# A mixed attention and mLSTM block: norms' row and gate columns through device memory, one turn for each small table

## The reference

```
h    = rms_norm(x, pre_norm_g)                       # one reciprocal norm for each token
proj = h @ w_in                                      # aq ak av az | mq mk mv mo mz | mi mf
ya   = moba_attention(partial_rope(aq), partial_rope(ak), av)
ya   = rms_norm(ya, attn_out_g) * silu(az)
qk   = silu(causal_depthwise_conv([mq, mk], conv_w, conv_b))
hm   = mlstm(q, k * 128**-0.5, mv, mi + i_bias, mf + f_bias)
       # lf = log_sigmoid(mf), running sums of lf, running maxima m_t,
       # weights exp(b_t - b_s + i_s - m_t), denominators max(|n q|, exp(-m_t))
ym   = sigmoid(mo) * layer_norm(hm) * mlstm_out_g * silu(mz)
x    = x + rms_norm([ya, ym] @ w_out, post_norm_g)
```

## Time and profile before

| | before |
|---|---|
| median of 3 runs | 317.78 us (317.5 to 318.87) |
| profiled execution: first to last instruction | 316.2 us |
| PE busy (matmul) | 309.4 us, 98% |
| DVE busy | 225.4 us, 71% |
| ACT busy | 165.2 us, 52% |
| POOL busy | 95.9 us, 30% |
| DMA, mean over the span | 121 GB/s |

### The profile page before, as it was taken

One profiled execution on the slowest core, in us unless ns is written; L12 is line 12 of the kernel. 1 busy time (PEld: TensorE's weight loads), 2 busy tenths in 40 slices (PEclk: granted clock), 3 DMA queues, 4 the chain that ended last, 5 costly groups with the idle time before them and its releaser, 6 DMA issues.

```text
span 316.2 us, 4992 instructions
## 1 busy us (share of the span) xinstructions
PE 309.4 (98%) x1599; PEld 256.4 (81%) x1599; DVE 225.4 (71%) x508; ACT 165.2 (52%) x336; POOL 95.9 (30%) x118
## 2 busy tenths in 40 slices
PE   8999999999999999999999999999999999999992
PEld 4888888888888888888888888778888888888882
DVE  2544999748998699968998568964577766856534
ACT  3548857287345324663157563384556876353301
POOL 8201006056350213002320025592711984000000
PEclk9999999999999999999999999999999999999999
DMA  7941553956725486645864332210220473310111
GB/s 222 323 99 38 153 149 93 170 163 150 134 68 146 134 158 205 188 124 122 180 227 151 102 90 77 73 66 31 67 68 0 125 200 145 133 68 0 68 66 67
DMA packets 29081, 38.30 MB, mean 121 GB/s; under 512 B 3624, under 2 KB 15184, under 8 KB 29056
## 3 DMA queue, kind: packets, MB, share of 16 engines
q1 hardware_dynamic: 27424, 34.51, 36.2%
q0 software_dynamic: 1472, 3.34, 7.0%
q10 hardware_dynamic: 160, 0.14, 0.1%
HBM read 33.68 MB, written 4.29 MB: 120 GB/s over the span
## 4 chain that ended last, share of the span: by engine, by line
PE 93%; issue 3%; DMA 2%; DVE 0%; DVEq 0%; SPq 0%; ACT 0%; POOLq 0%; POOL 0%; ACTq 0%
PE bank L1476 24%; PE bank L1478 24%; PE bank L1477 24%; PE bank L1814 3%; PE bank L1524 3%; PE bank L1758 3%; PE bank L1779 3%; PE bank L1612 2%; DMA farena<-in_x 2%; PE bank L1708 1%; PE bank L1505 1%; PE bank L1769 1%; PE bank L1613 1%; PE bank L1552 1%; PE bank L1551 1%
## 5 line engine op out<-in xcount | busy, mean ns | idle before, releaser
L778 ACT ACTIVATE w_hi<-w_raw 128x512 fp32r<-128x512 f32 x71 | 43.7, 626 | 63.2 <-PE bank L1478 51.1
L1476 PE MATMUL bank<-w_hi,xT_hi 128*128 128x512 f32 (+1 forms) x180 | 72.5, 403 | 0.0
L1478 PE MATMUL bank<-w_hi,xT_lo 128*128 128x512 f32 (+1 forms) x180 | 69.8, 388 | 0.0
L1477 PE MATMUL bank<-w_lo,xT_hi 128*128 128x512 f32 (+1 forms) x180 | 69.3, 385 | 0.0
L1043 DVE TENSOR_TENSOR w_lo<-w_raw,w_hi 128x512 fp32r<-128x512 f32 x64 | 45.5, 721 | 11.1 <-ACT w_hi L778 11.0
L1476 PE MATMUL bank<-xT_hi,w_hi 128*128 128x512 f32 x128 | 50.8, 397 | 0.0
L1478 PE MATMUL bank<-xT_hi,w_lo 128*128 128x512 f32 x128 | 50.1, 392 | 0.0
L1477 PE MATMUL bank<-xT_lo,w_hi 128*128 128x512 f32 x128 | 50.0, 390 | 0.0
L1478 PEld LDWEIGHTS bank<-w_hi,xT_lo 128*128 128x128 f32 x180 | 33.8, 188 | 7.2
L1476 PEld LDWEIGHTS bank<-w_hi,xT_hi 128*128 128x128 f32 x180 | 33.9, 188 | 5.8 <-issue 0.4
L1477 PEld LDWEIGHTS bank<-w_lo,xT_hi 128*128 128x128 f32 x180 | 34.0, 189 | 5.5
(11 more groups left out here) (211 smaller groups left out, 581.8 us busy)
## 6 DMA issues: line engine op xcount, KB each, us to landing
w_raw<-in_w_in SPq DMA_DIRECT2D x72, 256.0 KB, 2.9
w_raw<-in_w_out SPq DMA_DIRECT2D x16, 256.0 KB, 2.7
kq_rows<-stage SPq DMA_DIRECT2D x8, 256.0 KB
gy<-kq_rows SPq DMA_DIRECT2D x8, 256.0 KB, 3.5
gy<-in_x SPq DMA_DIRECT2D x4, 512.0 KB, 5.4
out_y<-gy SPq DMA_DIRECT2D x7, 256.0 KB, 2.1
farena<-in_x SPq DMA_DIRECT2D x4, 256.0 KB, 5.3
farena<-in_x SPq DMA_DIRECT2D x2, 512.0 KB, 7.5
```

The costliest lines, as they stand in the source:

```text
L778: a.activation(hi, raw, ACT.Copy).then_inc(w_hi_done, 1)
L1476: pe.matmul(o, hi, m_hi, start=start, stop=False)
L1477: pe.matmul(o, hi, m_lo, start=False, stop=False)
L1478: return pe.matmul(o, lo, m_hi, start=False, stop=stop)
```

## The change

Four things change, and no arithmetic on the result does.

1. **Norms' row.** PE turns `rx` (128 x 4) once into four rows, DVE copies 4 x 128 values, and POOL writes them to device memory, waits, and reads the row back into all partitions of `rbc`. `rbc_done` is now the landing of that DMA.
2. **Gate steps.** The multiplication of the gate rows by `rbc` (`gate_scale`) moves on DVE from ahead of slots 10 to 14 to step 8, behind the cuts of slots 12 to 14. ACT's three first gate steps (`gate_first`) move in the same way into step 8. PE waits for the small copy and no more for `rbc` before slot 10.
3. **Rotation table.** One turn of the whole table (128 x 128) takes the place of four; ACT's copy out of PSUM is 128 x 128; POOL writes it to device memory with four DMAs instead of one.
4. **Gate columns.** PE's four turns and DVE's copy are gone. SP, at slot 20, waits for the gate rows and issues five small DMAs to device memory; at slot 22 it waits for them and issues one DMA that reads back 32 values for each of 128 partitions, with neighbours 512 bytes apart in memory. ACT's exponential in step 18 and the decays wait for that DMA.

The semaphores' declarations and one repeated wait are left out of the diff.

```diff
@@ -87,6 +87,7 @@
 P_AT = [0, 512, 896, 1152]
 NU = NT * AH
+COLS_OUT, COLS_BACK = 20, 22
@@ -253,8 +254,8 @@
         pcol = sb("pcol", [P, R_END])
         wg_raw = sb("wg_raw", [P, NK, 8])
         wg = sb("wg", [P, NK, P], F32R)
-        aT = sb("aT", [P, NT, 16])
-        emt = sb("emt", [P, NT, MH])
+        gate_col = sb("gate_col", [P, 2 * NT * MH])
+        emt = sb("emt", [P, MH, NT])
         ssx = sb("ssx", [P, NT])
         msx = sb("msx", [P, NT])
         rx = sb("rx", [P, NT])
@@ -312,7 +313,7 @@
         bcol = pcol[0:16, R_BIAS:R_END]
         by_dims, whole = stage, gate
         rope_t = [f_part(F_COS, SEQ), f_part(F_SIN, SEQ)]
-        rope_flat = f_part(F_SIN, SEQ)[0:2 * ROT, :]
+        rope_flat = f_part(F_SIN, P)
         def by_block_order(ap):
             return ap.rearrange("p (m h j) -> p h m j", m=4, h=AH)
@@ -358,6 +359,8 @@
         kq_dram = nc.dram_tensor("kq_rows", (2, AH, DH, SEQ), F32, kind="Internal").ap()
         rope_dram = nc.dram_tensor("rope_rows", (2, ROT, SEQ), F32, kind="Internal").ap()
         g_dram = nc.dram_tensor("g_rows", (16, SEQ), F32, kind="Internal").ap()
+        rx_dram = nc.dram_tensor("rx_row", (1, SEQ), F32, kind="Internal").ap()
+        col_dram = nc.dram_tensor("col_rows", (2 * NT * MH, P), F32, kind="Internal").ap()
         x_in = [sem(f"x_in{c}") for c in range(len(X_CHUNKS))]
@@ -548,6 +553,19 @@
                 sp.dma_start(dst, src).then_inc(raw_in[n % RAW], 16)
                 if n == NK - 1:
                     sp.dma_start(wg_raw[:], w_in[0, :, MG:MG + 8].rearrange("(k p) c -> p k c", p=P)).then_inc(wg_in, 16)
+                if n == COLS_OUT:
+                    sp.wait_ge(gdiff_done, 1)
+                    sp.wait_ge(gneg_done, 1)
+                    for j in range(NT):
+                        rows_of_tile = slice(MH * j, MH * (j + 1))
+                        sp.dma_start(col_dram[rows_of_tile, :], gate_rows[rows_of_tile, j * P:(j + 1) * P])\
+                            .then_inc(cols_out, 16)
+                    sp.dma_start(col_dram[NT * MH:, :].rearrange("(h j) p -> h (j p)", j=NT), gate_rows[32:32 + MH, :])\
+                        .then_inc(cols_out, 16)
+                if n == COLS_BACK:
+                    sp.wait_ge(cols_out, 16 * (NT + 1))
+                    with nc.allow_non_contiguous_dma(reason="a column per row"):
+                        sp.dma_start(gate_col[:], col_dram.rearrange("g p -> p g")).then_inc(cols_back, 16)
                 if n == S_QK + 6:
                     sp.wait_ge(ssx_done, NT)
                     sp.dma_start(gains[:], attn_g.to_broadcast([P, AW])).then_inc(gain_in, 16)
@@ -637,6 +655,10 @@
             g.wait_ge(consts, 1)
             g.wait_ge(msx_done, 1)
             rsqrt(rx[:], msx[:]).then_inc(rx_done, 1)
+            g.wait_ge(rx_row_done, 1)
+            g.dma_start(rx_dram.rearrange("o (t p) -> (o t) p", p=P), rbc[0:NT, 0:P]).then_inc(rx_out, 16)
+            g.wait_ge(rx_out, 16)
+            g.dma_start(rbc[:], rx_dram.to_broadcast([P, SEQ])).then_inc(rbc_done, 16)
             g.wait_ge(gmax_done, 1)
             g.tensor_tensor(rows[4], rows[1], rows[2], ALU.subtract).then_inc(grows_done, 1)
@@ -680,8 +702,10 @@
             decay_rows(0)
             decay_mask(0)
             g.wait_ge(rope_flat_done, 1)
-            g.dma_start(rope_dram.rearrange("q j s -> (q j) s"), rope_flat).then_inc(rope_out, 16)
-            g.wait_ge(rope_out, 16)
+            for t in range(NT):
+                g.dma_start(rope_dram.rearrange("q j s -> (q j) s")[:, t * P:(t + 1) * P],
+                            rope_flat[t * 2 * ROT:(t + 1) * 2 * ROT, :]).then_inc(rope_out, 16)
+            g.wait_ge(rope_out, 16 * NT)
             for q in range(2):
                 g.dma_start(rope_t[q], rope_dram[q:q + 1].to_broadcast([AH, ROT, SEQ])).then_inc(rope_spread, 16)
             for t in range(NT):
@@ -816,16 +840,18 @@
             for t in range(NT):
                 mv_high(t)
-            a.wait_ge(gate_sb, 1)
-            a.activation(rows[0], gate_rows[32:48, :], ACT.Abs, bias=bcol[:, 1:2]).then_inc(absf_done, 1)
-            a.wait_ge(absf_done, 1)
-            a.activation(rows[1], rows[0], ACT.Exp, scale=-1.0).then_inc(expf_done, 1)
-            a.activation(rows[6], gate_rows[0:16, :], ACT.Identity, bias=bcol[:, 0:1]).then_inc(igate_done, 1)
+            def gate_first():
+
+                a.wait_ge(gate_sb, 1)
+                a.activation(rows[0], gate_rows[32:48, :], ACT.Abs, bias=bcol[:, 1:2]).then_inc(absf_done, 1)
+                a.wait_ge(absf_done, 1)
+                a.activation(rows[1], rows[0], ACT.Exp, scale=-1.0).then_inc(expf_done, 1)
+                a.activation(rows[6], gate_rows[0:16, :], ACT.Identity, bias=bcol[:, 0:1]).then_inc(igate_done, 1)
             def decays(h, j):
                 a.wait_ge(g_masked, NT * h + j + 1)
-                a.activation(decay[j], decay[j], ACT.Exp, bias=aT[:, j, 4 * j + h:4 * j + h + 1])\
+                a.activation(decay[j], decay[j], ACT.Exp, bias=gate_col[:, NT * j + h:NT * j + h + 1])\
                     .then_inc(decay_done, 1)
             def rope_scale():
@@ -838,7 +864,7 @@
             def rope_evac():
                 a.wait_ge(rope_ps, 1)
-                a.activation(rope_flat, bank[6][0:2 * ROT, :], ACT.Copy).then_inc(rope_flat_done, 1)
+                a.activation(rope_flat, bank[6][:, 0:P], ACT.Copy).then_inc(rope_flat_done, 1)
             def conv_silu(n):
                 a.wait_ge(conv_done, n + 1)
@@ -892,6 +918,7 @@
                         v_copy(t)
                 cut(b + AHEAD)
                 if b == S_QK:
+                    gate_first()
                     a.wait_ge(onep_done, 1)
                     a.activation(rows[0], rows[2], ACT.Ln).then_inc(ln_done, 1)
                 if b == S_QK + 1:
@@ -902,9 +929,8 @@
                     a.wait_ge(gmax_done, 1)
                     a.activation(gate_rows[32:48, :], rows[2], ACT.Copy, scale=-1.0).then_inc(gneg_done, 1)
                 if b == ST_AT[0]:
-                    a.wait_ge(aT_done, 1)
-                    a.activation(emt[:], bank[7][:].rearrange("p (t c) -> p t c", t=NT)[:, :, 32:32 + MH],
-                                 ACT.Exp).then_inc(emt_done, 1)
+                    a.wait_ge(cols_back, 16)
+                    a.activation(emt[:].rearrange("p h t -> p (h t)"), gate_col[:, NT * MH:], ACT.Exp)                        .then_inc(emt_done, 1)
                 for h in range(MH):
                     if b - 2 in PE_ST and PE_ST[b - 2][0] == h:
                         pm_high(*PE_ST[b - 2])
@@ -1085,18 +1111,21 @@
             v.tensor_scalar(rx_fourth[:], rx[:], 0.25, None, ALU.mult).then_inc(rx_half_done, 1)
             cut(RING)
             cut(RING + 1)
-            v.wait_ge(rbc_ps, 1)
-            v.tensor_copy(rbc[:], bank[5][:]).then_inc(rbc_done, 1)
-            v.wait_ge(rbc_done, 1)
+            v.wait_ge(rx_turned, 1)
+            v.tensor_copy(rbc[0:NT, 0:P], bank[5][0:NT, 0:P]).then_inc(rx_row_done, 1)
             v.wait_ge(par_done, 2)
             v.wait_ge(consts, 4)
             v.wait_ge(gate_split, 1)
             link(v.tensor_tensor(gate_rows, bank[7][0:P // 2, :], gate_low_rows, ALU.add))
-            v.tensor_tensor(gate_rows, gate_rows, rbc[0:P // 2, :], ALU.mult).then_inc(gate_sb, 1)
             cut(RING + 2)
             cut(RING + 3)
             for t in range(NT):
                 mv_low(t)
+
+            def gate_scale():
+
+                v.wait_ge(rbc_done, 16)
+                v.tensor_tensor(gate_rows, gate_rows, rbc[0:P // 2, :], ALU.mult).then_inc(gate_sb, 1)
             def gate_low():
@@ -1196,7 +1225,7 @@
                 for q in range(2):
                     v.bn_stats(bns[:, q, :], pv[:, q, 0:MD])
-                link(v.scalar_tensor_tensor(out=den[:], in0=pv[:, :, MD], scalar=-1.0, in1=emt[:, t0:t0 + 2, h],
+                link(v.scalar_tensor_tensor(out=den[:], in0=pv[:, :, MD], scalar=-1.0, in1=emt[:, h, t0:t0 + 2],
                                             op0=ALU.mult, op1=ALU.max))
                 link(v.tensor_tensor(den[:], pv[:, :, MD], den[:], ALU.max))
                 for q in range(2):
@@ -1271,15 +1300,12 @@
                     head_sum(*PE_PV[b - 2])
                 cut(b + AHEAD)
                 if b == S_QK:
+                    gate_scale()
                     gate_low()
                 if b == S_QK + 1:
                     gate_sums()
                 if b == S_QK + 2:
                     gate_maxima()
-                if b == S_QK + 6:
-                    v.wait_ge(gcol_ps, 1)
-                    v.tensor_copy(aT[:], bank[7][:].rearrange("p (t c) -> p t c", t=NT)[:, :, 0:16])\
-                        .then_inc(aT_done, 1)
                 for c in range(2):
                     for m in (2 * c, 2 * c + 1):
                         if b == S_AQ - 3 + (m > 0):
@@ -1562,25 +1588,13 @@
                 pe.wait_ge(rx_done, 1)
                 pe.wait_ge(xt_lo, NK)
```

(28 more changed lines are left out.)

## The result

| | before | after |
|---|---|---|
| median | 318.05 us (6 runs) | 325.31 us (6 runs, 324.4 to 327.15) |
| ratio of the runs | | 1.023, 95% interval 1.021 to 1.0251 |
| profiled execution, its span | 316.2 us | 325.4 us |
| profiled execution, its time | | 327.15 us |
| chain that ended last, share of PE | 93% | 79% |

The changed kernel is slower by 7.3 us, 2.3%. The forecast had the sign, the place and the chain of links, and half of the size (+3.6 us). The profiled execution is the slowest of the six, 1.8 us above their median, so its gap is larger than that of the median run. Of all executions behind the numbers of this document, one of ten of e3_rope_turn took 344.06 us at a mean granted clock of 0.851, and its ratio leaves that one out.

What follows compares the result with a forecast made beforehand. PE bounds the kernel, level with the gate chain at 69.7 us. Weighting end 69.62 + 2.3 (maxima) - 0.1 (copy gone) + 1.4 (columns) = 73.2, so +3.6: 321.4 us, range 318.9 to 325.5.

Steps and rivals of the forecast that it cites:

- the sign: Whole kernel: slower, median 317.78 + 3.6 = 321.4 us; slower given 0.80.
- the place: PE ahead of score tile 1 of head 0: waits some 4 us for the weighting of tile 0.
- the chain of links: Norms' row, gate steps, maxima, slot 24's issue and landing, ACT's decays, DVE's weighting: end moves from 69.62 to 73.2 us.
- The term of the sum for the gate columns: SP's queue at slot 22: the column read delays slot 24's landing by 1.4 us.
- the clock: Rival: PE idle about 4.5 us lets the clock fall, adding some 2 us, 323.5 us; chance 0.2, with costlier columns.
- the time at the rotation table: PE's turn after slot 11: may stall 0.5 us (none to 1.8), taken in by the later wait.
- T: Landing of the norms' row in `rbc` through device memory: 40.1 us, with ends 39.35 and 41.35.
- The maxima: DVE's gate maxima end at T+10.5, 50.6 us instead of 48.29, 2.3 us later.
- the wait is for T: Gate steps behind three slots: moving them costs those slots nothing and buys nothing.
- The small writes: SP at slot 20: five small DMAs at some 0.6 us each, slot 21 issued at 54.3 instead of 49.49.
- The column read: SP at slot 22: 4096 pieces of 4 bytes take 4 us of engine time, 1.4 of it delaying slot 24.
- Zero slack: Score tile 1 of head 0, kernel before: PE and the gate chain arrive together at 69.7 us.

Runs made afterwards that it cites:

- e3_rope_turn: Kernel before with only the rotation table's one turn: three PE turns fewer, four POOL writes instead of one; 317.79 us against 318.11.
- e7: Kernel before with only the gate steps moved behind slots 12 to 14 on DVE and ACT, norms' row still from PE's turns; 320.83 us, +3.0.
- e1: Kernel before with the norms' row through device memory and the gate steps moved; rotation table and gate columns turned as before; 322.51 us, +4.3.
- e4b: Kernel before with five small writes and an unused read of the same 16 KB as 128 rows of 128 bytes, PE's turns kept; 319.57 us, +1.4.
- e2: Kernel before with only the gate columns through device memory, without PE's four turns for them; 321.29 us, +3.1.
- e4a: Kernel before with the five small writes and the 4096-piece column read added, its result unused, PE's turns kept; 322.86 us, +4.7.
- e5: Kernel after with 26 idle matmuls on PE ahead of score tile 1 of head 0; 322.98 us, 2.3 us faster than after.
- e6: Kernel after with the gate-column read issued by ACT on its own queue in step 14; 325.25 us, the same as after.
- e11: e4a with the five small writes moved to slot 24 and the unused 4096-piece read to slot 27; 317.96 us against 317.87 before.

## Why the prediction was wrong in size

Two steps failed. The term of the sum for the gate columns, 1.4 us at slot 24, was too small: between the end of the maxima and the end of the weighting the change costs 2.5 to 3.6 us more than before. And the clock stood among the rivals and not in the sum, where it costs 2.3. This table has the two ends in each profiled execution:

| | maxima end | weighting ends | between |
|---|---|---|---|
| before | 48.29 | 69.62 | 21.33 |
| e7, steps moved | 49.88 | 71.14 | 21.26 |
| e1, norms' row and steps | 50.87 | 73.62 | 22.75 |
| e4b, small writes, harmless read | 47.91 | 71.08 | 23.17 |
| e2, columns | 48.68 | 72.43 | 23.75 |
| e4a, pieces unused | 48.16 | 72.44 | 24.28 |
| e5, after with the gap filled | 50.40 | 74.24 | 23.84 |
| e6, after with the read on ACT | 50.46 | 74.47 | 24.01 |
| after (its slowest execution) | 51.15 | 76.12 | 24.97 |
| forecast | 50.6 | 73.2 | 22.6 |

- **The place, the links and the sign** were right. The gap lies ahead of score tile 1 of head 0, ended by DVE's weighting behind ACT's decays behind slot 24; the time at the rotation table is a gap of 0.6 us (0.5 forecast) that adds nothing.
- **T** was 40.75 us in after and 40.1 in the forecast. The broadcast took 4.0 us, within the bounds and under the 4.55 that I had taken; the small write took 2.8 us, where I had taken the 1.9 of POOL's larger one. The two errors partly cancel, by luck.
- **The maxima** came at T + 10.4, as worked out (T + 10.5). But the reason was put wrong. I wrote that moving the steps costs the slots nothing and buys nothing, "because the wait is for T". e7 shows 1.6 us at the maxima and 3.0 us in all from the move alone. The two waits of DVE for ACT stood in my own sum, and I did not ask what they would be without the DMA.
- **The small writes** were costed by their issue on SP alone. With them POOL's write of the gate rows takes 1.0 us more, on the chain, and e4b, with them and a harmless read, has 1.8 us more than before between maxima and weighting. This term was missing. How much of the 1.8 is SP's wait and its later slots stays open.
- **The column read.** I charged 4 us of engine time, about what a quiet read of it takes (4.8 us in e11), and let 1.4 of it reach slot 24. Beside four broadcasts it took 10.8 to 12.4 us. Against e4b the pieces move the weighting of e4a by just those 1.4 us (1.1 from the maxima on), but that is luck: I had a far quicker read, and put the delay down to the order in SP's queue, and e6 shows that the same time is lost without that order. In all, slot 24 landed at 71.0 in after and at 69.3 in e6, where the forecast comes to 68.1. The estimate from the Trainium skill, DMA: Bandwidth & Descriptors, Bandwidth, 2.7 us for 256 pieces, takes the page's figure as one for each engine, which the page does not say; it is near e11, where 4.8 us less the 1.9 of the quickest DMA leave 2.9, and would have gone further wrong here.
- **The clock** was a rival with 4.5 us of idle time as its point, read off one row at the end of the kernel. In the profiled executions it fell after gaps of 6.6, 3.7, 3.0 and 2.0 us (after, e1, e4a, e7) and not after one of 3.0 (e2). One row gave a bound that was none.
- **What is missing** is 3.7 us. The clock is 2.3 of it, by e5. The chain is 1.0 to 1.3: in e5 and e6 the weighting ends that much behind the forecast's 73.2, and e6 has after's median. The profiled execution of after, 2.9 us behind it, shows more than the median run has.
- **Zero slack** at the earlier trace rows was one execution's picture. In e3 PE had no wait there.

By medians: moved steps 3.0, the norms' row on top of them 1.4, the columns 3.1, the rotation table -0.3; 7.2 of 7.3 us. Each holds its own share of lost clock, and with intervals of about 1 us to either side the close sum proves less than it seems. What stays open is the spread: in e1 the broadcasts lasted 11.9 us and slot 23 landed 11 us after issue, in e7, with nearly the same timing, 10.3 and 9.3. Whether the norms' row has to do with that wasn't found.

## What to carry to other kernels

Work taken off the busiest engine is worth nothing if the engine then waits, and the price of the replacement is read on the chain that it waits for. An order of steps that lets one engine compute while the other has other work is itself a resource: moving both halves to one place turns overlap into waits. A DMA's landing time belongs to the moment at which it is issued; the same one took 4.8 and 11.7 us. And a gap in PE is to be priced with what the clock takes after it, here some 2.3 us behind a gap of 5.7 us (e6).

## What the runs showed that I had not expected

- A read of 16 KB in 4096 pieces lands in 4.8 us alone and in 10.8 to 12.4 us beside four broadcasts of a row to 128 partitions; in 128 rows it takes 4.7 us beside them.
- With five writes of 2 to 8 KB to memory, issued within 2 us ahead of another queue's write of 32 KB, that one took 2.9 to 3.0 us in each of six kernels, and 1.9 in six without them (2.2 in e1).
- While the pieces were pending, SP's next issues took long: that of slot 23, right behind the read, 6.16 us in after, 5.86 in e2 and 7.84 in e5, where the median is 0.34. So slot 24 went out at 63.97 in after, with its buffer free at 62.11. With the read on ACT's queue slot 24 was issued in 0.35 us at 61.43, and landed 7.9 us later, so that it did not help.
- The granted clock fell to 1.2 GHz after a gap of 2.0 us in one execution and held through one of 3.0 us in another. The Trainium skill, TensorE: Matmul & The Clock Gate, Part 1, tells of a fall after idleness; the runs agree, and show that the length of the gap alone does not say whether it comes. Of the six executions of one kernel, e2, three show the loss in their mean granted clock and three do not.
